# Masks of the triangular inversion on VectorE, and the memory tokens turned by VectorE in runs of 32 columns instead of on TensorE

## The reference, cut to what matters

```
mkv = (rms_norm(mem, mem_norm_g) @ w_mem_kv).reshape(bsz, mlen, 2, MEM_HEADS, MEM_HEAD_DIM)
mem_k = rms_norm(mkv[:, :, 0], mem_k_norm_g)
mem_v = mkv[:, :, 1]
# layer 0: h = h + even_layer(h, ...): gated DeltaNet (8 heads of 128, chunks of 64 tokens), a Conformer
#          convolution (31 taps, LayerNorm) and attention into mem; one projection in, one out
#   sol = lax.linalg.triangular_solve(eye + a_mat, rhs, lower=True, unit_diagonal=True)   # per head and chunk
# layer 1: h = h + odd_layer(h, ...): stick-breaking attention (16 heads) and attention into mem
```

## Time and profile before

| | before |
|---|---|
| median of 3 runs | 1318.95 us (1318.78 to 1319.12) |
| profiled execution | 1318.3 us, its span 1316.5 us |
| TensorE busy | 1307.6 us, 99% of the span |
| VectorE, ScalarE, GpSimd busy | 994.1, 744.4, 103.6 us |
| granted TensorE clock | 1.00 of full speed |
| moved by DMA | 268.64 MB, mean 204 GB/s |

### The profile page before, as it was taken

One profiled execution on the slowest core, in us unless ns is written; L12 is line 12 of the kernel. 1 busy time (PEld: TensorE's weight loads), 2 busy tenths in 40 slices (PEclk: granted clock), 3 DMA queues, 4 the chain that ended last, 5 costly groups with the idle time before them and its releaser, 6 DMA issues.

```text
span 1316.5 us, 17502 instructions
## 1 busy us (share of the span) xinstructions
PE 1307.6 (99%) x6341; PEld 1099.1 (83%) x6341; DVE 994.1 (76%) x1541; ACT 744.4 (57%) x1165; POOL 103.6 (8%) x103
## 2 busy tenths in 40 slices
PE   9999999999999999999999999999999999999998
PEld 8898889888888888888888888888888888888887
DVE  5567589898898998676668477797788788667663
ACT  6556633476445556577336456748757558554341
POOL 2000301003020100000001020020110200000000
PEclk9999999999999999999999999999999999999999
DMA  9675465755756996656668655765765766967662
GB/s 315 203 210 181 143 196 155 198 176 160 229 168 194 308 281 198 217 185 215 208 192 267 220 177 164 234 193 170 230 205 159 238 195 184 282 214 227 196 193 80
DMA packets 175647, 268.64 MB, mean 204 GB/s; under 512 B 37920, under 2 KB 57801, under 8 KB 175561
## 3 DMA queue, kind: packets, MB, share of 16 engines
q1 hardware_dynamic: 172841, 262.81, 65.0%
q10 hardware_dynamic: 2720, 4.72, 1.1%
HBM read 249.00 MB, written 18.48 MB: 203 GB/s over the span
## 4 chain that ended last, share of the span: by engine, by line
PE 79%; DVE 1%; POOL 0%; issue 0%; DVEq 0%
PE job L1948 49%; PE job L1958 24%; PE mixer L2175 1%; PE mixer L2163 1%; PE mixer L1969 1%; PE mixer L2185 1%; PE mixer L2193 1%; PE mixer L2080 0%; PE mixer L2184 0%; PE mixer L2195 0%; PE mixer L2060 0%; DVE cvr L1695 0%; DVE wlo L1438 0%; PE mixer L2093 0%; PE mixer L2068 0%
## 5 line engine op out<-in xcount | busy, mean ns | idle before, releaser
L1948 PE MATMUL job<-whi,xhi 128*128 128x512 f32 x1628 | 648.6, 398 | 0.0
L1948 PE MATMUL job<-whi,xlo 128*128 128x512 f32 x1628 | 634.7, 390 | 0.0
L1438 DVE TENSOR_TENSOR wlo<-raw,whi 128x1024 fp32r<-128x1024 f32 x431 | 528.2, 1245 | 74.1 <-ACT whi L1087 73.2
L1087 ACT ACTIVATE whi<-raw 128x1024 fp32r<-128x1024 f32 x431 | 444.5, 1055 | 199.9 <-PE job L1958 162.0
L1958 PE MATMUL job<-wlo,xhi 128*128 128x512 f32 x1628 | 435.5, 389 | 0.0
L1958 PEld LDWEIGHTS job<-wlo,xhi 128*128 128x128 f32 x1628 | 305.6, 188 | 64.3
L1948 PEld LDWEIGHTS job<-whi,xhi 128*128 128x128 f32 x1628 | 305.9, 188 | 61.3
L1948 PEld LDWEIGHTS job<-whi,xlo 128*128 128x128 f32 x1628 | 306.0, 188 | 60.9
L1695 DVE SCALAR_TENSOR_TENSOR cvr<-cvr,vt 128x255 f32<-128x255 f32 (+14 forms) x240 | 106.2, 498 | 0.2
L1119 ACT ACTIVATE proj<-job,rstd 128x512 f32<-128x512 f32 x74 | 46.7, 683 | 63.1 <-PE job L1958 44.3
L1471 DVE TENSOR_TENSOR hid<-hid,job 128x512 f32<-128x512 f32 x46 | 29.5, 682 | 34.1 <-PE job L1958 34.1
(11 more groups left out here) (302 smaller groups left out, 984.4 us busy)
## 6 DMA issues: line engine op xcount, KB each, us to landing
raw<-in_od_w_in_dram SPq DMA_DIRECT2D x160, 512.0 KB, 4.6
raw<-in_ev_w_in_dram SPq DMA_DIRECT2D x143, 512.0 KB, 4.5
raw<-in_ev_w_out_dram SPq DMA_DIRECT2D x48, 512.0 KB, 5.5
raw<-in_od_w_out_dram SPq DMA_DIRECT2D x48, 512.0 KB, 5.2
raw<-in_w_mem_kv_dram SPq DMA_DIRECT2D x32, 512.0 KB, 4.6
proj<-turned_blocks SPq DMA_DIRECT2D x60, 128.0 KB, 4.4
turned_blocks<-proj SPq DMA_DIRECT2D x8, 512.0 KB, 4.7
turned_blocks<-mix SPq DMA_DIRECT2D x7, 512.0 KB, 5.4
```

The costliest lines, as they stand in the source:

```text
L1087: act(whi[:, c % RING, :, :], raw[:, c % RAWS, :, :], ACT.Copy).then_inc(s_hi, 1)
L1438: vec.tensor_tensor(wlo[:, c % RING, :, :], raw[:, c % RAWS, :, :], whi[:, c % RING, :, :].bitcast(F32), ALU.subtract).then_inc(s_lo, 1)
L1948: mm(pj[j % 2][n][:, :], x[:, s, cols], h, start=first, stop=False)
```

## The change

1. **Masks.** GpSimd's `d4x` is gone. VectorE masks instead (`masked`): the first level of both pairs in `inT`, ahead of its wait for `inD`, and each next level right behind the subtraction and the turn.
2. **Memory tokens.** `memx` now has partition 32 b + j, holding columns 512 b to 512 b + 511 of the tokens j, 32 + j, 64 + j, ... Each of the four loads fills 32 partitions. VectorE turns 32 x 32 blocks of it (`mt`, two k-tiles at a time, 8 steps) into `memt`. A k-tile then holds 32 columns of each quarter, not 128 neighbouring columns. ScalarE and VectorE make `xhi` and `xlo` from `memt`, and TensorE's transposes of `mem` are gone.
3. **What follows from that order.** The rows of `w_mem_kv` and the gains of `mem_norm_g` are read in the same order. A chunk of `w_mem_kv` is two transfers of 256 KB, each from a source of 4 x 32 rows into 128 partitions. The sums of squares are 8 of 512 columns, put together by 16 small copies and a reduction on VectorE.
4. **Times of steps.** The loads of `mem` and of `x` are spread out, the turns and gates of two jobs come 8 positions later, `rstd` 1 comes 6 later, the memory keys, queries and the attention into `mem` some 3 to 5 earlier, the last LayerNorm steps some 4 later. Taps move by a few. The shares of VectorE's time by which taps are placed grow for `inT` (0.55 to 1.0 of a chunk) and `d4y` (0.4 to 0.55), and `mt` gets 0.26.

In the diff, `do_d4x` and its mask go from GpSimd, `masked` and `do_mt` come to VectorE, `sc` is ScalarE's queue, and the last piece is TensorE's.

```diff
-    stream(3, p, [(("mload", b), 1.5) for b in range(4)])
+    stream(3, p, [(("mload", b), 3) for b in range(4)])
...
-    stream(3, oa, [(("xload", b), 1.5) for b in range(4)])
+    stream(3, oa + 2, [(("xload", b), 4) for b in range(4)])
...
-        memx = reg[:, :].rearrange("p (t d) -> p t d", t=T)
+        memx = reg[:, :].rearrange("p (a d) -> p a d", a=8)
+        memt = mflat[:, 4 * S:8 * S].rearrange("p (k s) -> p k s", k=4)
...
+                if name == "mem":
+                    for k in range(2):
+                        src = w[name][:, c0:c0 + 512].rearrange("(b k j) n -> k b j n", b=4, j=32)[2 * (c - CH0[j]) + k]
+                        sp.dma_start(raw[:, c % RAWS, k, :], src).then_inc(s_raw[c % RAWS], 16)
+                    return
...
-            def do_d4x(i):
...
-                nc.gpsimd.tensor_tensor(ofx[:, par, :, :], aq[:, 4 * par:4 * par + 4, 0, :],
-                                        level[:, l - BASE, :].unsqueeze(1).broadcast_to([128, 4, 128]), ALU.mult
-                                        ).then_inc(s_of[par], 1)
...
+            def masked(par, l):
+                vec.tensor_tensor(ofx[:, par, :, :], aq[:, 4 * par:4 * par + 4, 0, :],
+                                  level[:, l - BASE, :].unsqueeze(1).broadcast_to([128, 4, 128]), ALU.mult).then_inc(s_of[par], 1)
...
             def do_inT(g):
+                ve.wait_ge(s_const, 2)
+                for par in range(2):
+                    ve.wait_ge(s_aq, 4 * g + 2 * par + 2)
+                    if g:
+                        ve.wait_ge(s_t[par], LEVELS + 1)
+                    masked(par, BASE)
                 ve.wait_ge(s_inD, 16 * g + 16)
...
                         ins = vec.transpose(tinvt[b:b + 32, par, :, b + 32:b + 64], tinv[b + 32:b + 64, par, :, b:b + 32])
...
+                masked(par, l + 1)
...
+            def do_mt(p):
+                ve.wait_ge(s_min, 64)
+                ve.wait_ge(s_xl, F_OA + 8 if p < 2 else F_MEM + 2 * p - 2)
+                vec.transpose(memt[:, 2 * (p % 2):2 * (p % 2) + 2, :].rearrange("p k s -> p (k s)"),
+                              memx.rearrange("p a (k j) -> p k a j", j=32)[:, 2 * p:2 * p + 2]).then_inc(s_jt, 1)
...
-                sc.dma_start(memx[:, :, 512 * b:512 * b + 512],
-                             mem[:, 512 * b:512 * b + 512].rearrange("(t p) d -> p t d", p=128)).then_inc(s_min, 16)
+                sc.dma_start(memx[32 * b:32 * b + 32], mem[:, 512 * b:512 * b + 512].rearrange("(a j) d -> j a d", j=32)
+                             ).then_inc(s_min, 16)
...
             def do_xt(n):
-                if F_H <= n < F_H + 12:
+                if F_MEM <= n < F_H + 12:
                     return
```

## The result

The changed kernel takes 1396.32 us (median of 4 runs, 1395.96 to 1396.67), the kernel before 1319.03 us in the same series: ratio 1.0584, 95% interval 1.057 to 1.0597, so 77 us slower. Forecast were 1415 us, with 1382 to 1440 as the range of the case that came true and 1372 to 1455 as the whole range.

The account below looks back on a forecast made before the run. TensorE was taken as the bound, busy 1307.6 of 1316.5 us. Late w_mem_kv loads move chunk 192 from 609.4 to 709 us: 709 + (1318.3 - 609.4) - 3.1 = 1415 us, range 1372 to 1455.

Parts of the forecast that it names:

- the case that came true: Loads of w_mem_kv carried by four DMA engines: 80 in 100, likeliest 1415 us.
- Four engines: Loads of w_mem_kv: a source of 4 groups leaves 4 of 16 engines, 186 us of loads where TensorE needs 87.
- signs named in advance: TensorE idle some 100 us between 510 and 710, landings 10 to 30 us, DMA share 0.25 to 0.35, masks 0.6 to 0.8 us.
- The rate: Loads of w_mem_kv: 22.6 GB/s for each engine, 186 us in all; bounds 20.0 and 25 GB/s.
- The estimate beside it: Loads of w_mem_kv at the fabric's ceiling, 27.2 GB/s per engine: 154 us of loads, run of 1382 to 1396 us.
- The tail: From the last w_mem_kv landing at 690 us to chunk 192 at 709: 19.5 us of landing, splits, scores and chunks.
- SyncE's holes: SyncE's waits for turned-block writes idle the engines: 10 to 40 us on top, 1425 to 1455; above 1455, 5 in 100.
- Transposes of mem: TensorE between 487 and 535 us: 16 pairs removed at 0.27 us each, 4.3 us in all, vanishing in the wait.
- The turns: Turning mem on VectorE: 8 turns at 0.71 us, 5.7 us, plus some 2 us of small steps; nothing on the path.
- Masks: Inversion: 12 masks on VectorE at 0.71 us, 8.5 us, hidden; TensorE's 0.5 us wait goes, its 1.6 us "issue" wait stays.
- The LayerNorm's sum: No term of its own; moved steps were taken to cost TensorE what they cost before.
- the first rival: All engines carry the w_mem_kv loads, which stay hidden: 1314.1 us; 12 in 100.

Follow-up runs that it names:

- e2: Changed kernel with the source of each w_mem_kv load ordered as 32 rows x 4 groups instead of 4 groups x 32 rows: 1316.39 us, one run.
- e3: Changed kernel with the source of each w_mem_kv load cut into 8 groups of 16 rows instead of 4 of 32: 1319.97 us, one run.
- e8: Changed kernel with the source of each w_mem_kv load cut into 2 groups of 64 rows instead of 4 of 32: 1559.23 us, one run.
- e4: Kernel before with only the w_mem_kv loads changed, to 64 transfers of 256 KB from 4 groups of 32 rows: 1390.66 us, one run.
- e1: Changed kernel with each w_mem_kv chunk loaded by four 128 KB transfers, one per quarter, 32 partitions each: 1314.21 us, ratio 0.996 to the kernel before.
- e9: Changed kernel with write and read of the two turned results of w_mem_kv issued by ScalarE on its own queue, not SyncE: 1396.25 us.
- e5: e1 with the LayerNorm's sum on TensorE, and the steps behind it, one position later: 1312.32 us, ratio 0.9949 to the kernel before.
- e6: Kernel before with only the masks of the inversion moved to VectorE: 1316.35 us, ratio 0.9983.
- e10: e6 with GpSimd also computing the first two masks at the old place, results unused: 1317.99 us, one run.

## Why the prediction was right, step by step

**Four engines: right, and the step that decided.** e2, e3 and e8 move the time by the number of groups alone, e4 brings it about by itself, e1 takes it away, and the packets in flight are as many as the theory says. Of the signs named in advance, the share (0.26), the rate (102 GB/s, 80 to 100 named), the long landings (13.8 to 15.4 us for four of the loads in the chain that ended last), the late splits and remainders and the masks at 0.68 us came; TensorE's idle time is 72.6 us, not some 100.

**But one ground for it was wrong.** I had argued from the issue durations of the earlier trace rows that the work of issuing follows the entries of the slowest dimension. The quickest issues with 2, 4, 8 and 32 in that place took 528, 521, 588 and 534 ns: they don't follow it. A row of before spoke against it already: a load of 512 KB with 128 there took 0.37 us, less than the 421 ns with 16. The rule that held is the one cited from the Trainium skill; the row put in front of it told nothing about the engines. As far as my own rows go, four engines was a lucky choice.

**The rate: mis-sized.** I took 22.6 GB/s for an engine, from the fullest stretch with 16; 25.8 was measured, close to the 25 that I had worked out of the landing times and used as the bound. Loads alone are then 64 x 2.54 = 163 us where I had 186. The first was issued 3.6 us earlier than I took (489.38), and exchanges, landing and the start took 20 us where I had 11: the last load landed at 672.4 us, forecast 690. The estimate beside it, for 27.2 GB/s, was added up wrongly: 154 us of loads are 32 us less than 186, so it is 1383 us, or 1369 with the 14 us; 1382 to 1396 belong to 25 GB/s.

**The tail: right in sum.** From the last landing to chunk 192 it took 20.2 us, forecast 19.5. The last read of turned blocks waited 12.5 us behind queued loads, but landed at 674.5, 2.1 us after the last load, where I had 3. The chain that ended last shows it (start, us, what):

```profile
646.54 12.26 DMA turned_blocks<-mix
658.82 1.90 SPq L912
...
661.96 12.54 DMA proj<-turned_blocks
```

ScalarE then needed 7.3 us, forecast 8, and from the second scores to chunk 192 it was 10.7 us, forecast 8.4, because of the clock (below). Chunk 192 began at 692.60, forecast 709:

```profile
692.60 0.58 PE L1990 MATMUL job<-whi,xhi 128*128 128x512 f32 x1
```

Behind it 702.0 us follow, forecast 704.0 (1316.5 - 609.4 - 3.1). So -16.4 and -2.0 make the 18.4 us between the sum and the profiled run (1414.8 and 1396.4), and nearly all of the -16.4 stems from the loads.

**SyncE's holes: seen, but worth nothing.** The 4.2 us for a read and 2.4 us for a write are there, and up to 1.3 us of waiting between. e9 took them all out of SyncE's queue and the time stayed: the four engines were full anyway (e9 above).

**Transposes of mem: right.** From chunk 149 on most pairs gave back 0.25 to 0.27 us. e5 against e6, which differ by the memory tokens, the steps moved with them and the sum, is 1310.4 against 1314.6, 4.2 us; forecast were 4.3. The turns are 0.71 us each as taken, the 16 small copies 0.16 us each where I had 0.1, and both were hidden in e5.

```profile
L1500 DVE STREAM_TRANSPOSE mix<-reg x8: 704/710/722, 482.7 to 542.5; 128x512 f32<-128x512 f32 x8
```

**Masks: price right, gain too small.** A mask is 0.68 us at the median, 0.71 taken. I had said that the 1.6 us of "issue" stay. They fell to 0.5, because the first mask of GpSimd no longer slows VectorE (e10). e6 won 1.9 us of span instead of 0.5 (2.5 us between the medians, 0.9 to 3.4 by the interval).

**The LayerNorm's sum: missed.** A cost of 1.7 us that I had at nothing ("its steps cost TensorE what they cost before"): the moved plan put this sum right behind GpSimd's last two additions, of which the first took 3.9 us in e1 instead of 0.74 (last section). e5 against e1, which differ by this place alone, is 1310.4 against 1312.9 us of span. So it is partly luck that e1 took 1314.2 us, the very price of the first rival (1314.1): the masks gave more and the sum took it back.

**TensorE's clock** I had left out. Right behind the pause of 20.1 us it was granted at 0.50, the lower of the two levels (1.2 of 2.4 GHz), and soon at 1.00 again:

```profile
681.80:685.60 3.80, 3.75 (x9) 3.03 (x10) 3.58 (x9) 3.77 (x8) 0.00 (x0) 0.50 0.19 35
...
690.00:692.60 2.60, 2.60 (x14) 2.22 (x13) 2.56 (x7) 2.60 (x6) 0.00 (x0) 1.00 0.55 173
```

The second scores took 3.75 us there, the third 1.89. In the tail this cost 2.3 us; over the starved stretches, with 0.85 on average from 520 to 600 us, the pace was that of the loads.

## What to carry to other kernels

When the source of a transfer is regrouped, look at its slowest dimension as well as at bytes and run lengths: 2, 4 or 8 entries there left 2, 4 or 8 of 16 DMA engines at work here, and putting the larger dimension first, or cutting the transfer so that each part has 32, brought the others back. In a profile the sign is a low DMA share together with issues that take microseconds. And a step that moves from GpSimd to VectorE can pay twice, since what GpSimd no longer does may have stretched VectorE's own work.

## What the runs showed of the hardware that was not expected

One engine moved 25.8 GB/s, the same with 2 and with 4 engines at work; the fullest stretch of 16 has 22.6 for each. Two queues did not add to that: 102 GB/s from one and from two. In the queue with such loads a write of 512 KB took 12.2 us to land at the median, and 6.0 us from another queue. GpSimd slows VectorE's operation on 128x256 from 0.37 to 0.85 us, and in e1 one of GpSimd's additions to `lnacc` took 3.9 us while VectorE made three remainders, where 0.74 is the median:

```profile
L1032 POOL TENSOR_TENSOR lnacc<-lnacc,cvr x7: 722/741/3907, 243.4 to 546.4; 128x256 f32<-128x256 f32 x7
```
